# A block kernel on one core: the six inverse levels on 64 by 64 diagonal blocks instead of whole 128 by 128 matrices

## The reference, cut to what matters

```
def step(state, inp):                       # RWKV-7, one token, per head
    r_t, w_t, k_t, v_t, kk_t, a_t = inp
    sk = jnp.einsum('bhij,bhj->bhi', state, kk_t)
    state = (state * w_t[:, :, None, :]
             - sk[..., None] * (kk_t * a_t)[:, :, None, :]
             + v_t[..., None] * k_t[:, :, None, :])
    return state, jnp.einsum('bhij,bhj->bhi', state, r_t)
...
gate_a, gate_b = jnp.split(jax.nn.sigmoid(pg), 2, axis=-1)
y = gate_a * (o_a @ w_proj_a) + gate_b * (o_b @ w_proj_b)
```

## Time and profile before

| | |
|---|---|
| median of 3 runs | 1070.8 us (1068.94 to 1071.31) |
| the profiled execution, its own time | 1071.18 us |
| its span, first to last instruction | 1069.0 us |
| PE busy | 1060.4 us, 99% of the span |
| PE weight loads (PEld) | 955.6 us, 89% |
| DVE, ACT, POOL busy | 68%, 59%, 44% |
| mean granted TensorE clock | 0.997 |
| the six levels on PE | 125.05 to 152.57 us |

### The profile page before, as it was taken

The page is one execution under the profiler, slowest core; times in us unless marked ns, Lnnn a source line. Parts: engine busy times, 40 slices in busy tenths (PEclk is TensorE's granted clock), DMA queues, the critical chain, the costliest instruction groups (busy, mean ns, idle before and its releaser), DMA issues.

```text
span 1069.0 us, 22130 instructions
## 1 busy us (share of the span) xinstructions
PE 1060.4 (99%) x7104; PEld 955.6 (89%) x7104; DVE 725.5 (68%) x1549; ACT 627.8 (59%) x1188; POOL 472.3 (44%) x224
## 2 busy tenths in 40 slices
PE   9999999999999999999999999999999999999997
PEld 8998899999998888889999999998888888888886
DVE  7764761545539999877888888865555555555554
ACT  6763464555565555657777777764455444555444
POOL 4684523687138889787777777740000000000000
PEclk9999999999999999999999999999999999999999
DMA  7462302356545555555444444445555555555553
GB/s 267 169 207 99 118 22 80 123 189 223 178 136 179 191 183 194 178 177 178 158 157 156 150 154 151 156 158 195 196 194 187 192 193 196 196 191 191 190 193 137
DMA packets 52130, 181.20 MB, mean 169 GB/s; under 512 B 5811, under 2 KB 7859, under 8 KB 51964
## 3 DMA queue, kind: packets, MB, share of 16 engines
q1 hardware_dynamic: 51660, 180.13, 49.6%
q10 hardware_dynamic: 432, 0.55, 0.1%
HBM read 179.60 MB, written 1.06 MB: 169 GB/s over the span
## 4 chain that ended last, share of the span: by engine, by line
PE 82%; POOL 9%; issue 7%; DVE 1%; DMA 0%; POOLq 0%; ACT 0%; ACTq 0%; DVEq 0%
PE PS L839 11%; PE PS L841 11%; PE PS L840 11%; PE PS L414 11%; PE PS L415 10%; PE PS L416 10%; POOL lo L1270 9%; PE PS L425 4%; PE PS L426 2%; PE PS L790 1%; PE PS L791 1%; PE PS L619 1%; PE PS L627 1%; PE PS L574 1%; PE PS L606 1%
## 5 line engine op out<-in xcount | busy, mean ns | idle before, releaser
L1270 POOL TENSOR_TENSOR lo<-raw,hi 128x1024 fp32r<-128x1024 f32 x191 | 461.5, 2422 | 205.3 <-ACT hi L890 192.7
L890 ACT CAST hi<-raw 128x1024 fp32r<-128x1024 f32 x331 | 346.3, 1047 | 190.6 <-DMA raw<-in_v_units 170.7
L1318 DVE TENSOR_TENSOR lo<-raw,hi 128x1024 fp32r<-128x1024 f32 x140 | 171.6, 1226 | 156.6 <-ACT hi L890 156.6
L414 PE MATMUL PS<-xb,hi 128*128 128x256 f32 x776 | 226.7, 292 | 0.3 <-issue 0.3
L415 PE MATMUL PS<-xb,hi 128*128 128x256 f32 x776 | 219.9, 283 | 0.0
L416 PE MATMUL PS<-xb,lo 128*128 128x256 f32 x776 | 219.8, 283 | 0.0
L425 PE MATMUL PS<-xb,hi 128*128 128x512 f32 x576 | 203.4, 398 | 0.9 <-POOL lo L1270 0.7
L839 PE MATMUL PS<-hi,xb 128*128 128x512 f32 x512 | 199.7, 390 | 0.2 <-issue 0.2
L841 PE MATMUL PS<-lo,xb 128*128 128x512 f32 x512 | 199.4, 389 | 0.0
L840 PE MATMUL PS<-hi,xb 128*128 128x512 f32 x512 | 199.4, 389 | 0.0
L426 PE MATMUL PS<-xb,lo 128*128 128x256 f32 x576 | 160.9, 279 | 0.0
(11 more groups left out here) (295 smaller groups left out, 1436.4 us busy)
## 6 DMA issues: line engine op xcount, KB each, us to landing
raw<-in_u_units SPq DMA_DIRECT2D x128, 512.0 KB, 3.2
raw<-in_v_units SPq DMA_DIRECT2D x128, 512.0 KB, 3.2
raw<-in_w_in_units SPq DMA_DIRECT2D x43, 512.0 KB, 3.3
raw<-in_w_q_units SPq DMA_DIRECT2D x16, 512.0 KB, 3.3
raw<-in_w_proj_units SPq DMA_DIRECT2D x8, 512.0 KB, 3.3
raw<-in_w_out_units SPq DMA_DIRECT2D x8, 512.0 KB, 3.3
arena<-bias_rows SPq DMA_DIRECT2D x2, 512.0 KB, 5.0
arena<-in_subkeys_t SPq DMA_DIRECT2D x1, 1024.0 KB, 6.2
```

The lines of the kernel that those rows point to most:

```text
L414: mm(ps, hi[:, s, c], mh[:, k, :], start=(k == k0), stop=False)
L890: nc.scalar.copy(hi[:, j, :], raw[:, j, :]).then_inc(hi_made, 1)
L1270: nc.gpsimd.tensor_tensor(lo[:, w, :], raw[:, w, :], hi[:, w, :].bitcast(F32), ALU.subtract).then_inc(lo_pool, 1)
L1318: V.tensor_tensor(lo[:, w, :], raw[:, w, :], hi[:, w, :].bitcast(F32), ALU.subtract).then_inc(lo_dve, 1)
```

## The change

Each 128 by 128 inverse is now held as its two 64 by 64 diagonal blocks, one on rows 0 to 63 and one on rows 64 to 127, so all level buffers have 64 columns. A level works on two groups of four squares; every product is two 64 by 64 ones, `half_rows(0)` and `half_rows(1)`, in opposite corners of the array. The flip is a plain product with the identity instead of a transpose. Five levels work inside the blocks; the sixth makes the off-diagonal block from the products with the diagonal ones, and its result goes to `VA` and half of `VT[1]`. The right sides (L653, L657 before) and the solution (L666 before) are made in halves of 64 output rows. In the solution one half needs only 64 input rows and the other all 128.

Gate units 31 and 32 move into the levels: 16 steps (`gate_part`) of 3 matmuls, one behind each of the three products of a level, until they are used up. All later gate units move up by two places, so four instead of six stand ahead of the projections. On ACT, `gate_copy(39, 40)` stands before `output_high` and `gate_copy(41, 42)` behind it, where it was 37 to 39 and 40 to 42.

```
+            units(30)
+
+            def gate_part(step):
+
+                g, k = 31 + step // KT, step % KT
+                ps, c = PS[:, unit_bank(g), 0:T], slice(P * k, P * k + P)
+                if k == 0:
+                    splits_ready(g, lo_pool, g + 1 - LO_FIRST)
+                if k == 0 and g == 31:
+                    pe.wait_ge(halves_in, len(WIDE))
+                elif k == 0:
+                    pe.wait_ge(act_evac, copied(30))
+                mm(ps, hi[:, g % 4, c], xh[:, k, :], start=(k == 0), stop=False)
+                mm(ps, hi[:, g % 4, c], xl[:, k, :], start=False, stop=False)
+                last = mm(ps, lo[:, g % 4, c], xh[:, k, :], start=False, stop=(k == KT - 1))
+                if k == KT - 1:
+                    last.then_inc(unit_done, 1)
+
+            def level_block(bank, q, i, d):
...
             for lv in range(len(LEVELS)):
-                for q in range(4):
-                    pe.wait_ge(flip_sb, 4 * lv + q + 1)
-                    for i in range(2):
-                        last = mm(PS[:, q, P * i:P * i + P], S8[:, 2 * q + i, :], W8[:, 2 * q + i, :], start=True, stop=True)
-                    last.then_inc(p1_ps, 1)
+                turned_over = lv + 1 == len(LEVELS)
+                for q in range(2):
+                    if lv:
+                        pe.wait_ge(x_sb, 2 * (lv - 1) + q + 1)
+                    for i in range(4):
+                        for d in range(2):
+                            last = mm(level_block(2, q, i, d), WT[half_rows(d), 4 * q + i, :],
+                                      ident[half_rows(d), half_rows(d)], start=True, stop=True)
+                    last.then_inc(flip_ps, 1)
+                if 3 * lv < 2 * KT:
+                    gate_part(3 * lv)
                 if lv == 0:
                     pe.wait_ge(sc_sb, HEADS)
-                    pe.wait_ge(act_evac, copied(30))
-                for q in range(4):
-                    pe.wait_ge(p1_sb, 4 * lv + q + 1)
-                    for i in range(2):
-                        last = mm(PS[:, 4 + q, P * i:P * i + P], P1[:, 2 * q + i, :], VT[lv % 2][:, 2 * q + i, :],
-                                  start=True, stop=True)
+                for q in range(2):
+                    pe.wait_ge(flip_sb, 2 * lv + q + 1)
+                    for i in range(4):
+                        for d in range(2):
+                            inputs = mats[half_rows(d), 8 * q + 4 * d + i, 2, half_rows(1 - d)] if turned_over else S8[half_rows(d), 4 * q + i, :]
+                            last = mm(level_block(4, q, i, 1 - d if turned_over else d), inputs, W8[half_rows(d), 4 * q + i, :],
+                                      start=True, stop=True)
+                    last.then_inc(p1_ps, 1)
+                if 3 * lv + 1 < 2 * KT:
+                    gate_part(3 * lv + 1)
+                for q in range(2):
+                    pe.wait_ge(p1_sb, 2 * lv + q + 1)
+                    for i in range(4):
+                        for d in range(2):
+                            last = mm(level_block(6, q, i, 1 - d if turned_over else d), P1[half_rows(d), 4 * q + i, :],
+                                      VT[lv % 2][half_rows(d), 4 * q + i, :], start=True, stop=True)
                     last.then_inc(x_ps, 1)
-                if lv + 1 < len(LEVELS):
-                    for q in range(4):
-                        pe.wait_ge(x_sb, 8 * lv + 2 * q + 2)
-                        flip(q)
+                if 3 * lv + 2 < 2 * KT:
+                    gate_part(3 * lv + 2)
...
+                    for b in (0, HD):
+                        m, value = 8 * n + c + b // 16, vtok[:, n, P * c + b:P * c + b + HD]
+                        for d in range(2):
+                            o = PS[half_rows(d), 2 + b // HD, HD * c:HD * c + HD]
+                            last = mm(o, mats[:, m, 0, half_rows(d)], value, start=True, stop=(n == 0), skip_group_check=True)
...
+                            for d in range(2):
+                                o = PS[half_rows(d), 2 + b // HD, HD * c:HD * c + HD]
+                                last = mm(o, keys[:, half_rows(d)], ST[b:b + HD, b // HD, c, :], start=False, stop=True,
+                                          skip_group_check=True)
...
-                units(31 + 3 * n)
+                units(33 + 3 * n)
                 pe.wait_ge(g_sb, n + 1)
-                pe.wait_ge(x_sb, 8 * len(LEVELS))
+                pe.wait_ge(x_sb, 2 * len(LEVELS))
                 for m in range(8):
-                    inverse = (VT[len(LEVELS) % 2] if chunk_head(m)[1] else WT)[:, 4 * n + m % 4, :]
-                    last = mm(PS[:, 4, HD * m:HD * m + HD], inverse, Gs[:, HD * m:HD * m + HD], start=True, stop=True)
+                    i, h = 4 * n + m % 4, m // 4
+                    for d in range(2):
+                        o = PS[half_rows(d), 4, HD * m:HD * m + HD]
+                        if d == h:
+                            last = mm(o, WT[half_rows(d), i, :], Gs[half_rows(d), HD * m:HD * m + HD], start=True, stop=True)
+                        else:
+                            last = mm(o, (VT[1] if h else VA)[:, i, :], Gs[:, HD * m:HD * m + HD], start=True, stop=True)
                 last.then_inc(sk_ps, 1)
                 p_turned(6 * n, 6 * n + 1)
-                units(32 + 3 * n)
+                units(34 + 3 * n)
...
-            for n in range(4 * len(LEVELS)):
-                act.wait_ge(flip_ps, n + 1)
-                q = n % 4
-                nc.scalar.copy(W8[:, 2 * q:2 * q + 2, :].rearrange("p a b -> p (a b)"), PS[:, q, 0:T]).then_inc(flip_sb, 1)
-                if 4 <= n < 20 and q == 3:
-                    for e in range(n - 7, n - 3):
+            for lv in range(len(LEVELS)):
+                for q in range(2):
+                    act.wait_ge(flip_ps, 2 * lv + q + 1)
+                    nc.scalar.copy(W8[:, group(q), :], level_banks(2, q)).then_inc(flip_sb, 1)
+                if 1 <= lv <= 4:
+                    for e in range(4 * lv - 4, 4 * lv):
                         exponential(e % HEADS, e // HEADS)
+                if lv == 3:
+                    gate_copy(31)
+            gate_copy(32)
...
-            gate_copy(37, 38, 39)
+            gate_copy(39, 40)
             output_high(0)
             output_high(1)
-            gate_copy(40, 41, 42)
+            gate_copy(41, 42)
...
+                    if size >= HD // 2:
+                        pool.wait_ge(kept, columns_kept(lv, q) - (2 if size < HD else 1))
+                    if size == HD:
+                        nc.gpsimd.tensor_copy(VA[half_rows(1), group(q), :], VT[1][half_rows(1), group(q), :]).then_inc(kept, 1)
+                    elif size == HD // 2:
+                        nc.gpsimd.tensor_copy(half_block(new, 0, 1), half_block(old, 0, 1)).then_inc(kept, 1)
+                        pool.wait_ge(kept, columns_kept(lv, q) - 1)
+                        nc.gpsimd.tensor_copy(half_block(new, 1, 1), half_block(old, 1, 1)).then_inc(kept, 1)
+                    else:
+                        nc.gpsimd.tensor_copy(crossing(new, size), crossing(old, size)).then_inc(kept, 1)
+            pool.wait_ge(kept, columns_kept(len(LEVELS) - 1, 1))
...
+                for q in range(2):
+                    dve.wait_ge(p1_ps, 2 * lv + q + 1)
+                    if size == HD:
+                        V.tensor_copy(P1[:, group(q), :], level_banks(4, q)).then_inc(p1_sb, 1)
+                    else:
+                        across = con[:, C_LV + HD * lv:C_LV + HD * lv + HD].unsqueeze(1).to_broadcast([P, 4, HD])
+                        V.tensor_tensor(P1[:, group(q), :], level_banks(4, q), across, ALU.mult).then_inc(p1_sb, 1)
+                for q in range(2):
+                    dve.wait_ge(x_ps, 2 * lv + q + 1)
+                    dve.wait_ge(kept, columns_kept(lv, q))
+                    w, change = WT[:, group(q), :], level_banks(6, q)
+                    old, new = VT[lv % 2][:, group(q), :], VT[(lv + 1) % 2][:, group(q), :]
+                    if size == HD:
+                        V.tensor_scalar(VA[half_rows(0), group(q), :], change[half_rows(0)], -1.0, None, ALU.mult)
+                        V.tensor_scalar(old[half_rows(1)], change[half_rows(1)], -1.0, None, ALU.mult).then_inc(x_sb, 1)
+                    elif size == HD // 2:
+                        for d in range(2):
+                            V.tensor_tensor(half_block(w, d, 1), half_block(old, d, 1), half_block(change, d, 1), ALU.subtract)
+                            last = V.tensor_tensor(half_block(new, d, 0), half_block(old, d, 0), half_block(change, d, 0),
+                                                   ALU.subtract)
+                        last.then_inc(x_sb, 1)
+                    else:
+                        V.tensor_tensor(crossing(w, size), crossing(old, size), crossing(change, size), ALU.subtract)
```

(54 more changed lines are left out.)

82 lines of the change are left out of this document (26 added, 56 removed).

## The result

The changed kernel takes 1072.89 us (median of 20 runs, 1071.22 to 1074.17), the kernel before 1070.66 (20 runs, 1068.94 to 1072.83). The ratio is 1.0022, with a 95% interval from 1.0016 to 1.0028: slower by some 2.2 us, 0.2%, which is small but clear of no change. The profiled execution took 1073.22 us, its span is 1071.4.

What follows compares the result with a forecast made beforehand. PE's own stream was taken as the bound. Savings of 4.2 and 1.25 less losses of 4.5 and 1.75 gave -0.8, so 1071.6 from the median 1070.8; with half a clock loss it said 1072.0, range 1064.5 to 1076.

Steps and rivals of the forecast that it cites:

- A: In the solutions, changes of shape drain PE; 1072.0 us in all, range 1069.5 to 1075; chance 0.62.
- Bound: Whole kernel: PE holds 82% of the chain and the levels wait for nothing, so only PE instructions' time counts.
- Levels: Six levels: 29.1 us, 5.8 of it moved gate-unit work; net 23.3 against 27.5, 4.2 saved.
- Right sides: Right sides ahead of the solutions: 0.6 us saved in chunk 0, 0.65 in chunk 1 (3.07 for 3.73), 1.25 together.
- Solution: Solutions of both chunks: 0.26 us a product from alternating shapes, 4.0 a chunk instead of 1.74, 4.5 lost.
- Rival B: Solutions: no drain between halves on different columns, 1.0 us saved there; 1064.5 to 1067 in all; chance 0.27.
- End of the mixer: Ahead of unit 43: PE waits for POOL's low part, late because ACT's casts come first; 1.75 us lost.
- The clock: Lower clock, 3.4 us costing 1.7 before, may fall at the solutions; half a loss more counted.
- Rival C: Levels lose the clock or their pairs; 1077 to 1092 us in all; chance 0.11.
- serial pairs: Levels: pairs writing one PSUM bank run in turn, 1.86 us a product, 16.7 lost, 1088; 0.02 of Rival C's 0.11.

Runs made afterwards that it cites:

- e1: Changed kernel with each solution's 16 products in two rows of one shape, neighbours alternating corners or column halves: 1065.5 us, ratio 0.9952 to the kernel before.
- e5: On top of e1 and e3 together, right sides of chunk 1 and outputs also ordered by shape: 1060.83 us, ratio 0.9916 to the kernel before.
- e7: On top of e1 and e3 together, a level's three gate-unit steps in one piece behind x: 1061.82 us, ratio 0.9919 to the kernel before.
- e6: On top of e1 and e3 together, all 16 gate-unit steps ahead of the levels, none inside: 1063.66 us, ratio 0.9936 to the kernel before.
- e2: Like e1 on the changed kernel, but neighbouring products mostly in the same corner or column half: 1066.09 us, ratio 0.9959 to the kernel before.
- e3: Changed kernel with ACT making the high part of unit 43 before the output casts: 1070.32 us, ratio 0.9997 to the kernel before.

## Why the prediction was right

Forecast 1072.0 (1064.5 to 1076), measured 1072.89; the case is A, the likeliest. Step by step:

- *Bound.* PE's own stream. Right: every edit that took us from it gave them back in the time (e1, e5, e7), and the one that turned changes of shape into as many waits changed nothing (e6).
- *Levels.* 29.1 forecast, 29.02 in the trace. The pairs run, and the gain of 4.3 is there. The waits behind the level of size 32 were 0.7 where 0.4 was reckoned; changes of shape at 0.33 a step instead of 0.35 made up for it.
- *Right sides.* 1.25 forecast, 1.7 measured: chunk 1 took 2.63, not 3.07 (chunk 0 took 1.08, as reckoned). The term was mis-sized because it counted the products on all four corners of the array as two at a time, see below.
- *Solution.* 4.0 forecast, 4.03 and 3.86 measured, 0.26 a product. e1 and e2 show the cause: the same products take 1.23 in rows of one shape. Rival B, no drain between halves on different columns, is out. The Trainium skill ("TensorEngine Tiling (Array Packing)", Key Properties) says that changing the tiling mode drains TensorE; the trace agrees, also where the neighbour's columns are others, with 0.14 to 0.15 us a change here.
- *End of the mixer.* 1.75 forecast, 1.67 in the row (1.83 from where unit 43 could have followed), with the releasers that were named; e3 shows it by taking it away.
- *The clock.* Half a loss more than before was to be counted, one whole came: 6.8 us at 1.2 GHz instead of 3.4, behind both solutions. The forecast has a slip here: 1071.6 and half a loss, 0.85, make 1072.4 and not 1072.0. With the half loss in full it would have been 0.4 low, with the whole one 0.4 high. Shown is that the low clock goes with the alternating solutions: the profiles of the changed kernel and of e3 have 6.8 us of it there, those of the seven kernels with grouped solutions none. It does not follow every one of them, as e3 kept the clock behind its second. Why it falls there stays open: in e6 PE waits over a fifth of the levels and keeps it. Rival C, the levels losing the clock, did not come, in any profile; nor did the serial pairs: L638 takes 0.93 and not 1.86. The Trainium skill's rule on row tiles and one PSUM bank ("TensorEngine Tiling (Array Packing)", Gotcha 1) does not hold for pairs on different partitions of the bank; the measurement decides.

The luck in it should be seen too. Four terms, 4.2 and 1.25 saved and 4.5 and 1.75 lost, gave a sum under 1, so a small error in any of them could have turned its sign. The right sides came out 0.45 better than forecast and the clock some 1.3 worse than the number has it, and these two partly cancel. The change to smaller products was a gain by itself, and two details, the order of 16 products and the place of one cast, hid it. Undone, they leave 1063.6.

## What to carry to other kernels

Small products that use a half or a quarter of the array are cheap in long rows of one shape and dear one by one: order a stage by the shape of its products first, by head or column second, and let the first product of a bank alone open it. Work moved into gaps is only a gain if the gaps are longer than the two changes of shape around it, 0.33 us here. And when units are taken away from between two stages, walk back from the next unit's split to the instruction that its maker stands behind, as the cover is thinner by just those units.

## What the runs showed of the hardware that was not expected

The products of the right sides that use 64 rows and 64 columns in all four corners of the array (L692 in e5) are 32 records, and from the first of them at 169.00 to the next stretch at 169.63 are 0.63 us. One change of shape at 0.15 is in it, so 0.48 is left for 32, 0.015 a record. In two corners 32 records take 0.93 (L638), 0.029 a record. So four corners run side by side as two do, near 0.06 for a set of four. The levels use two corners only; whether their products can be laid on all four was not tried.
